# Hybrid trunk step on one Trainium2 core: each 1 MB piece of w_mod asked for as four transfers of 512 columns

## The chip, the cores and the metric

The kernel runs on 1 core of one Trainium2 chip. Its engines are TensorE (in the profile PE, and PEld for its weight loads), VectorE (DVE), ScalarE (ACT), GpSimd (POOL) and SyncE (SP), which here only asks for transfers. 16 DMA engines move the data. The time is the device time of one execution in microseconds; three runs of the kernel before gave 1928.62 to 1929.17, median 1928.89.

## The reference

One inference step of a two-layer trunk over two groups of tokens (128 context tokens, 512 latent tokens, 1024 features) in float32. Layer 0 mixes by windowed attention and a gated DeltaNet in both directions, layer 1 by latent attention; each is followed by a convolution FFN. All norms are modulated by a map of the conditioning vector:

```python
def trunk_layer(l, x, cvec, prm, ctx):
    mod = jax.nn.silu(cvec) @ prm["w_mod"][l] + prm["b_mod"][l]
    shift1, scale1, gate1, shift2, scale2, gate2 = jnp.split(mod, N_MOD, axis=-1)
    h = rmsnorm(x, prm["norm_pre"][l, 0]) * (1.0 + scale1) + shift1
    ...                                   # mix: even_mixer (l = 0) or odd_mixer (l = 1)
    x = x + gate1 * rmsnorm(mix, prm["norm_post"][l, 0])
    h = rmsnorm(x, prm["norm_pre"][l, 1]) * (1.0 + scale2) + shift2
    f = conv_ffn(h, prm["ffn_w_up"][l], prm["ffn_conv"][l], prm["ffn_w_down"][l])
    return x + gate2 * rmsnorm(f, prm["norm_post"][l, 1]), new_ctx
```

`w_mod` is (2, 1024, 6144): 50 MB, the largest tensor. The DeltaNet of layer 0 runs in chunks with a triangular inverse in each:

```python
    t_inv = lax.linalg.triangular_solve(a + eye, eye, left_side=True, lower=True, unit_diagonal=True)
    u = t_inv @ (vc * bc[..., None])
    w = t_inv @ (kb * jnp.exp(gc)[..., None])
```

## The kernel before, in words

The order of all work is written out by hand for each engine; engines meet by semaphores. Activations lie with features on partitions, tokens along the row. Weight blocks of 128 output columns come through two raw buffers, are split into a high and a low part by ScalarE and VectorE, and TensorE multiplies three times per block (`proj`, L2007).

`w_mod` is worked on in two places. The first 2048 columns of layer 0 (`w_mod_first`, eight pieces, one per 128 input rows) come at the start. The other 10240 columns, five rounds of eight pieces, are spread over the delta steps, from 229 to 431 us. A piece is 128 partitions by 2048 columns, a row of 8 KB, thus 1 MB. Four buffers `MW` (`w_mod_raw`) lie in the memory of the raw weight buffers, free in that stretch. Piece u goes to buffer u % 4. SyncE (`mod_load`, L626 to L631) waits until TensorE is done with piece u - 4 (`mod_done`) and asks for it in one transfer, which adds 16 to `mod_landed{u % 4}` when all of it is there. The first eight pieces of the program have added 16 to the same semaphores once.

TensorE uses a piece with silu(c) as the weights: `mod_part` (L2211) in one go, four matmuls of 512 columns; `mod_half` (L2220) in two halves of four times 256. These stand as filler between the steps of the delta ladder. There are five delta rounds r, each with two chains c (forward and backward), and in each a ladder of levels `lv` that inverts the triangular matrix: TensorE multiplies 64 x 64 blocks (L2398, then L2451 and L2454), VectorE masks and adds (L1700, L1706, L1709), TensorE goes on. `mod_first_half` waits for a piece and does one half between L2398 and L2451; `mod_piece(halved=True)` does the other after L2454. In rounds 1 to 4 three whole pieces stand together at the start of the round, so three slots come free within 2 us and SyncE asks for three pieces there. The code of this stretch has no loops: each instruction stands once in memory. After the last piece SyncE asks for the blocks of `ev_w_out`.

Of the kernel before, what the change touches and what calls it, by code (L numbers as in the profile page):

```python
# [27 lines left out]
D = 1024  # L28
KD = D // P
# [79 lines left out]
def build(nc, a, outs):  # L109
# [14 lines left out]
    def S(name):  # L124
        if name not in sems:
            sems[name] = stack.enter_context(nc.semaphore(name))
        return sems[name]
# [41 lines left out]
    def place(name, shape, off, dt=F32):  # L169
        return nc.alloc_sbuf_tensor_at(name, [P] + shape, dt, offset=BASE + 4 * off)  # L170
# [121 lines left out]
    MSLOTS = 4  # L292
    MW = [place(f"w_mod_raw{s}", [2 * D], R_RAW + s * 2 * D) for s in range(MSLOTS)]
# [154 lines left out]
    def mod_columns_of(i):  # L448

        return (i + 1) // 3, 2 * D * ((i + 1) % 3)  # L450
# [105 lines left out]
    with stack:  # L556
# [4 lines left out]
        def _(sp):  # L561
# [39 lines left out]
            wm = [a["w_mod"][l].rearrange("(k p) m -> p k m", p=P) for l in range(2)]  # L601
# [24 lines left out]
            def mod_load(u):  # L626

                if u >= MSLOTS:
                    sp.wait_ge(S("mod_done"), KD + u - MSLOTS + 1)
                l, m0 = mod_columns_of(u // KD)  # L630
                sp.dma_start(MW[u % MSLOTS][:, :], wm[l][:, u % KD, m0:m0 + 2 * D]).then_inc(S(f"mod_landed{u % MSLOTS}"), 16)  # L631
            for u in range(MSLOTS):
                mod_load(u)
            for u in range(MSLOTS, MPARTS):
                mod_load(u)
# [1364 lines left out]
        def _(pe):  # L2000
# [207 lines left out]
            def mod_part(w, k, b):  # L2208

                for j in range(4):  # L2210
                    last = pe.matmul(PS[32 * j:32 * j + 32, b * 512:b * 512 + 512], SCX[:, k, :], w[:, 512 * j:512 * j + 512],  # L2211
                                     start=(k == 0), stop=(k == KD - 1))
                last.then_inc(S("mod_done"), 1)

            def mod_half(w, k, b, x):

                n = 2 * P
                for j in range(4):
                    c0 = 512 * j + n * x
                    last = pe.matmul(PS[32 * j:32 * j + 32, b * 512 + n * x:b * 512 + n * x + n], SCX[:, k, :], w[:, c0:c0 + n],  # L2220
                                     start=False, stop=(k == KD - 1 and x == 1))
                if x == 1:
                    last.then_inc(S("mod_done"), 1)

            def mod_turn(n, rows, b):

                pe.wait_ge(S("mod_rows"), n)
                for j in range(4):
                    last = turn(PS[:, b * 512 + P * j:b * 512 + P * j + P], rows[:, P * j:P * j + P])
                last.then_inc(S("mod_turned"), 1)  # L2230
# [75 lines left out]
            def mod_first_half(r, k):  # L2306

                u = KD * r + k
                pe.wait_ge(S(f"mod_landed{u % MSLOTS}"), 16 * (u // MSLOTS + 2))
                mod_half(MW[u % MSLOTS], k, 6, 0)  # L2310

            def mod_piece(r, k, halved=False):

                u = KD * r + k
                if k == 0 and r > 0:
                    pe.wait_ge(S("a_rotated"), r)
                    mod_turn(r + 1, MROW, 7)
                if halved:
                    mod_half(MW[u % MSLOTS], k, 6, 1)
                else:  # L2320
                    pe.wait_ge(S(f"mod_landed{u % MSLOTS}"), 16 * (u // MSLOTS + 2))
                    mod_part(MW[u % MSLOTS], k, 6)

            def v_turn(x):
# [45 lines left out]
            for r in range(NT):  # L2370
# [30 lines left out]
                if r == 0:  # L2401
                    v_turn(0)
                else:
                    for c in range(2):
                        pe.wait_ge(*both("eg", c, r + 1))
                    for k in range(3):
                        mod_piece(r, k)
                for lv in range(LEVELS - 1):
# [24 lines left out]
                    if lv == 0:  # L2433
                        if r == 0:
                            mod_piece(r, 0)
                        continue
                    if lv in (4 + e, 5 + e) and r < NT - 1:
                        k_times_state(r, lv - 4 - e)
                    elif r == 0 and lv < 5 or r > 0 and lv < 4:
                        mod_first_half(r, lv + 2 * (1 - e))  # L2440
# [16 lines left out]
                    if r == 0 and lv < 5 or r > 0 and lv < 4:  # L2457
                        mod_piece(r, lv + 2 * (1 - e), halved=True)
                    elif r == 0:
                        mod_piece(r, 5)  # L2460
                    elif lv == 4:
                        mod_first_half(r, 6)
                    else:
                        mod_piece(r, 6, halved=True)
# [15 lines left out]
                if r == 0:  # L2480
                    k_times_state(r, 1)
                else:
                    mod_first_half(r, LEVELS)
# [328 lines left out]
```

## Time and profile before

| | |
|---|---|
| median of 3 runs | 1928.89 us (1928.62 to 1929.17) |
| the profiled execution: its time | 1928.23 us |
| its span, first to last instruction | 1926.4 us |
| granted TensorE clock, mean | 0.993 |
| TensorE busy | 1841.1 us, 96% of the span |
| VectorE, ScalarE, GpSimd busy | 963.8, 827.9, 55.0 us |
| transfers `w_mod_raw<-in_w_mod` | 40 of 1024 KB, median 6.9 us to landing |
| read from HBM, written | 165.08 MB, 3.44 MB |

The profile is of one execution. "Busy" counts the union of an engine's instructions; a matmul's end is modelled. A wait "<- issue" is idle time of an engine that no semaphore in the profile explains. A wait "<- DMA" was ended by a transfer that landed. The DMA share is the mean busy share of the 16 DMA engines; in a short window it can pass 1.00, since a packet counts in the window in which it starts. A packet is what one DMA engine moves as one piece of contiguous memory.

### The profile page before, as it was taken

To read this page: it belongs to the slowest core of one execution; us is meant where nothing else is said; L and a number is where in the kernel's file an instruction comes from. 1 tells how busy PE (TensorE), PEld (TensorE's weight loads), DVE (VectorE), ACT (ScalarE), POOL (GpSimd) and SP (SyncE) were. 2 spreads that over 40 slices of the span, in tenths; PEclk is the share of its full clock that TensorE was granted. 3 is DMA by queue.
4 is the path that set the end of the run, shared out by engine and by line. 5 is a ranking of instruction groups with operands and counts; after the bars stand their busy time and mean duration, and the time that the engine had idled before them with its cause. 6 is when DMAs were issued, how large, how long until landed. Compare 5 with 4: busy or idle time off the path is not lost.

```text
span 1926.4 us, 36263 instructions
## 1 busy us (share of the span) xinstructions
PE 1841.1 (96%) x14824; PEld 1698.8 (88%) x14824; DVE 963.8 (50%) x1613; ACT 827.9 (43%) x1420; POOL 55.0 (3%) x76
## 2 busy tenths in 40 slices
PE   6999998888899999999999999999999999999998
PEld 3999966667799999999999887776899999999997
DVE  4433355556746655235555743344375553255555
ACT  4545422225745544124445653343464441244453
POOL 0000122220000000000000000000000000000000
PEclk9999999998999999999999999999999999999999
DMA  7222366531021223222234311110211232122243
GB/s 284 65 58 66 128 252 221 199 141 51 1 71 44 77 71 87 71 66 68 73 94 140 95 44 32 27 35 28 67 44 55 76 87 78 55 76 76 78 136 115
DMA packets 238723, 170.23 MB, mean 88 GB/s; under 512 B 20139, under 2 KB 230285, under 8 KB 232333
## 3 DMA queue, kind: packets, MB, share of 16 engines
q1 hardware_dynamic: 238604, 168.54, 28.2%
q8 instruction: 88, 1.44, 0.3%
q14 instruction: 31, 0.25, 0.0%
HBM read 165.08 MB, written 3.44 MB: 87 GB/s over the span
## 4 chain that ended last, share of the span: by engine, by line
PE 85%; DVE 6%; ACT 4%; issue 3%; DMA 1%; SPq 0%; ACTq 0%; DVEq 0%
PE ps L2007 46%; PE ps L2083 15%; PE ps L2040 4%; PE ps L2201 3%; PE ps L2708 2%; PE ps L2745 2%; PE ps L2704 2%; PE ps L2398 1%; PE ps L2220 1%; PE ps L2578 1%; PE ps L2451 1%; PE ps L2555 1%; PE ps L2211 1%; PE ps L2028 1%; ACT w_hi L782 1%
## 5 line engine op out<-in xcount | busy, mean ns | idle before, releaser
L782 ACT ACTIVATE w_hi<-w_raw 128x1024 fp32r<-128x1024 f32 (+4 forms) x187 | 198.6, 1062 | 559.6 <-PE ps L2007 436.0
L1366 DVE TENSOR_TENSOR w_lo<-w_raw,w_hi 128x1024 fp32r<-128x1024 f32 (+4 forms) x191 | 234.2, 1227 | 377.2 <-ACT w_hi L782 376.8
L2007 PE MATMUL ps<-h_hi,w_hi 128*128 128x322 f32 x1648 | 381.5, 313 | 3.2 <-ACT conv L972 1.7
L2007 PE MATMUL ps<-h_lo,w_hi 128*128 128x322 f32 x1648 | 380.2, 312 | 0.0
L2007 PE MATMUL ps<-h_hi,w_lo 128*128 128x322 f32 x1648 | 378.1, 310 | 0.0
L2007 PEld LDWEIGHTS ps<-h_hi,w_hi 128*128 128x128 f32 x1648 | 278.1, 189 | 4.8 <-ACT conv L1192 2.0
L2007 PEld LDWEIGHTS ps<-h_hi,w_lo 128*128 128x128 f32 x1648 | 279.1, 189 | 0.0
L2007 PEld LDWEIGHTS ps<-h_lo,w_hi 128*128 128x128 f32 x1648 | 279.1, 189 | 0.0
L2083 PE MATMUL ps<-g_hi,w_hi 128*128 128x322 f32 x352 | 110.7, 314 | 2.7 <-DVE g_lo L1850 1.6
L2083 PE MATMUL ps<-g_lo,w_hi 128*128 128x322 f32 x352 | 109.6, 311 | 0.0
L2083 PE MATMUL ps<-g_hi,w_lo 128*128 128x322 f32 x352 | 109.1, 310 | 0.0
L2083 PE MATMUL ps<-h_hi,w_out_hi 128*128 128x322 f32 x288 | 90.8, 315 | 0.0
L2083 PE MATMUL ps<-h_lo,w_out_hi 128*128 128x322 f32 x288 | 89.8, 312 | 0.0
L2083 PE MATMUL ps<-h_hi,w_out_lo 128*128 128x322 f32 x288 | 89.5, 311 | 0.0
L1837 DVE SCALAR_TENSOR_TENSOR conv<-u,vec_cols,conv 128x642 f32<-128x642 f32 x88 | 78.0, 886 | 12.5 <-ACT conv L1192 12.1
L1840 DVE SCALAR_TENSOR_TENSOR conv<-u,vec_cols,conv 128x642 f32<-128x642 f32 x88 | 78.1, 887 | 10.6 <-DVE conv L1837 0.6
L1197 ACT ACTIVATE g_hi<-gated 128x642 f32 (+1 forms) x44 | 32.6, 741 | 104.0 <-DVE gated L1848 104.0
L2083 PEld LDWEIGHTS ps<-g_hi,w_hi 128*128 128x128 f32 x352 | 66.3, 188 | 4.0 <-DVE g_lo L1850 2.2
L1192 ACT ACTIVATE conv<-ps,vec_cols 128x644 f32<-128x644 f32 x88 | 69.7, 792 | 0.0
L2083 PEld LDWEIGHTS ps<-g_lo,w_hi 128*128 128x128 f32 x352 | 66.4, 189 | 0.2
L2083 PEld LDWEIGHTS ps<-g_hi,w_lo 128*128 128x128 f32 x352 | 66.5, 189 | 0.0
L1868 DVE COPY f_t<-ps 128x644 f32 (+1 forms) x16 | 13.3, 829 | 100.9 <-PE ps L2007 82.3
(376 smaller groups left out, 3337.5 us busy)
## 6 DMA issues: line engine op xcount, KB each, us to landing
w_raw<-in_ffn_w_up SPq DMA_DIRECT2D x88, 512.0 KB, 3.7
w_mod_raw<-in_w_mod SPq DMA_DIRECT2D x40, 1024.0 KB, 6.9
w_raw<-in_ffn_w_down SPq DMA_DIRECT2D x48, 704.0 KB, 4.5
w_raw<-in_ev_w_in SPq DMA_DIRECT2D x18, 512.0 KB, 3.6
w_mod_first<-in_w_mod SPq DMA_DIRECT2D x8, 1024.0 KB, 15.6
w_raw<-in_ev_w_out SPq DMA_DIRECT2D x8, 512.0 KB, 4.3
w_raw<-in_od_w_out SPq DMA_DIRECT2D x8, 512.0 KB, 4.0
w_raw<-in_od_w_kv_up SPq DMA_DIRECT2D x24, 128.0 KB, 2.3
```

The source lines that it names most:

```text
L782: act.activation(WH[slot][:, 0:k, :], RAW[slot][:, 0:k, :], ACT.Copy).then_inc(w_hi, 1)
L1192: act.activation(halves(Y[b][:, :]), pair(b0 + 2 * slot), ACT.Copy, scale=vcol(v0 + b * FCH, j)).then_inc(evac_a, 1)
L1366: dve.tensor_tensor(WL[slot][:, 0:k, :], RAW[slot][:, 0:k, :], WH[slot][:, 0:k, :].bitcast(F32), ALU.subtract).then_inc(w_lo, 1)
L1837: dve.scalar_tensor_tensor(y[:, 1:643], u[:, 0:642], vcol(v0 + b * FCH, j), y[:, 1:643], ALU.mult, ALU.add).then_inc(S(f"f_conv{b}"), 1)
L1840: last = dve.scalar_tensor_tensor(y[:, 1:643], u[:, 2:644], vcol(v0 + b * FCH + 4 * FCH, j), y[:, 1:643], ALU.mult, ALU.add)
L2007: last = pe.matmul(out, w_of(k, wi), x_of(k, xi, i), start=(k == 0 and p == 0), stop=(k == ks - 1 and p == 2))
L2040: last = pe.matmul(bank(2 * slot + hf, HW), (WH, WL)[wi][slot][:, k, :], x[xi][:, k, hf * HW:(hf + 1) * HW], start=(k == 0 and p == 0), st ...
L2083: last = pe.matmul(out, w[wi][:, k, :], x[xi][:, k, tk(g)], start=(k == 0 and p == 0), stop=(k == ks - 1 and p == 2))
L2201: return pe.transpose(out, src, IDENT[0:rows, 0:rows])
L2704: return pe.matmul(area(s, k0, w), QPE[i % 2][half(s), tile], KPT[half(s), k0:k0 + w], start=True, stop=False)
L2708: return pe.matmul(area(s, k0, w), QN[h][:, tile], KN[h][:, k0:k0 + w], start=False, stop=True)
L2745: last = pe.matmul(COUT[:, P * s:P * s + P], VO[i % 2][:, s, kt_tile, :], pt, start=(x == 0), stop=(x == len(tiles) - 1))
```

## The change

`mod_load` asks for a piece in four transfers of 512 columns each (a row is then 2 KB), into the same buffer. All four add 16 to the piece's semaphore, so a piece adds 64, and TensorE's two waits count accordingly. The pieces of the first eight (`w_mod_first`) stay as they are, and so does every instruction of TensorE, VectorE, ScalarE and GpSimd.

```diff
--- before.py
+++ after.py
@@ -628,7 +628,9 @@
                 if u >= MSLOTS:
                     sp.wait_ge(S("mod_done"), KD + u - MSLOTS + 1)
                 l, m0 = mod_columns_of(u // KD)
-                sp.dma_start(MW[u % MSLOTS][:, :], wm[l][:, u % KD, m0:m0 + 2 * D]).then_inc(S(f"mod_landed{u % MSLOTS}"), 16)
+                for j in range(4):
+                    sp.dma_start(MW[u % MSLOTS][:, 512 * j:512 * j + 512], wm[l][:, u % KD, m0 + 512 * j:m0 + 512 * j + 512]
+                                 ).then_inc(S(f"mod_landed{u % MSLOTS}"), 16)
             for u in range(MSLOTS):
                 mod_load(u)
             for u in range(MSLOTS, MPARTS):
@@ -2306,7 +2308,7 @@
             def mod_first_half(r, k):
 
                 u = KD * r + k
-                pe.wait_ge(S(f"mod_landed{u % MSLOTS}"), 16 * (u // MSLOTS + 2))
+                pe.wait_ge(S(f"mod_landed{u % MSLOTS}"), 16 + 64 * (u // MSLOTS + 1))
                 mod_half(MW[u % MSLOTS], k, 6, 0)
 
             def mod_piece(r, k, halved=False):
@@ -2318,7 +2320,7 @@
                 if halved:
                     mod_half(MW[u % MSLOTS], k, 6, 1)
                 else:
-                    pe.wait_ge(S(f"mod_landed{u % MSLOTS}"), 16 * (u // MSLOTS + 2))
+                    pe.wait_ge(S(f"mod_landed{u % MSLOTS}"), 16 + 64 * (u // MSLOTS + 1))
                     mod_part(MW[u % MSLOTS], k, 6)
 
             def v_turn(x):
```

## Rows read from the trace of the kernel before

**Rows 1.** The page: all packets; the instruction queue: packets, MB, share.
```profile
DMA packets 238723, 170.23 MB, mean 88 GB/s; under 512 B 20139, under 2 KB 230285, under 8 KB 232333
q8 instruction: 88, 1.44, 0.3%
```

**Rows 2.** Waits of TensorE, 225 to 445 us: who <- what: us, times, longest.
```profile
PE ps L2454 <- issue: 5.0, 4, 1.7
PE ps L2220 <- issue: 2.2, 2, 1.2
PE ps L2398 <- issue: 1.4, 1, 1.4
PE ps L2211 <- DMA w_mod_raw<-in_w_mod: 1.0, 1, 1.0
PE ps L2451 <- issue: 0.8, 1, 0.8
PE ps L2220 <- DMA w_mod_raw<-in_w_mod: 0.3, 1, 0.3
```

**Rows 3.** Chain that ended last, 225 to 445 us: start, us, what.
```profile
229.81 8.92 DMA w_mod_raw<-in_w_mod
289.00 1.71 issue
415.56 1.18 issue
```

**Rows 4.** Timeline at 291.2 us: start, us, instruction [idle before <- what ended it].
```profile
291.18 0.29 DVE L1706 TENSOR_TENSOR r_blocks<-r_blocks,ps 128x128 f32<-128x128 f32 x1 [1.96 <-PE ps L2454]
```

**Rows 5.** Instruction queue in the 0.1 us from 288.4, 414.4 and 421.98: packets, MB, share.
```profile
q8 instruction: 1, 0.02, 60.1%
...
q8 instruction: 1, 0.02, 54.9%
...
q8 instruction: 1, 0.02, 62.4%
```

**Rows 6.** Windows: length, PE PEld DVE ACT POOL busy (xcount), PEclk, DMA share, GB/s.
```profile
234.00:241.50 7.50, 6.20 (x189) 3.92 (x189) 3.85 (x12) 4.89 (x14) 6.76 (x6) 1.00 1.01 426
1921.00:1922.00 1.00, 0.68 (x6) 0.68 (x7) 0.27 (x1) 0.00 (x0) 0.00 (x0) 1.00 1.07 412
34.50:36.00 1.50, 1.50 (x12) 0.21 (x8) 0.06 (x1) 1.38 (x2) 0.00 (x0) 0.50 1.14 346
285.27:289.05 3.78, 3.73 (x140) 2.69 (x134) 2.19 (x9) 0.00 (x0) 2.88 (x3) 1.00 1.01 425
411.80:415.60 3.80, 3.74 (x126) 2.70 (x125) 1.97 (x8) 0.00 (x0) 2.92 (x3) 1.00 1.02 349
416.74:421.30 4.56, 4.55 (x125) 2.87 (x127) 1.33 (x4) 0.00 (x0) 0.00 (x0) 1.00 0.31 115
```

**Rows 7.** Queues and issues in 405 to 409.6 us; all packets in 280 to 288.4.
```profile
q1 hardware_dynamic: 154, 1.15, 70.4%
q8 instruction: 1, 0.02, 1.2%
w_mod_raw<-in_w_mod SPq DMA_DIRECT2D x3, 1024.0 KB, 7.7
...
DMA packets 383, 2.88 MB, mean 343 GB/s; under 512 B 32, under 2 KB 32, under 8 KB 32
```

**Rows 8.** SyncE's issues (start, us), then a wait of its in the whole run.
```profile
8.09 3.96 SPq L603 DMA_DIRECT2D w_mod_first<-in_w_mod  x8
...
SPq L631 <- PE ps L2220: 95.5, 20, 8.9
```

**Rows 9.** Pieces: all 40 to landing; the one of 280.05; its first use.
```profile
DMA to landing us min/median/max: 4.7/6.9/12.6
...
DMA to landing us min/median/max: 5.1/5.1/5.1
...
287.43 0.42 PE L2220 MATMUL ps<-w_mod_raw,silu_c 128*32 128x256 f32 x4
```

## The prediction

> **What bounds the kernel now.** I read the page first: a span of 1926.4 us and TensorE busy for 96% of it and 40 transfers `w_mod_raw<-in_w_mod` of 1 MB each (all in the table above). A change in how these land can only matter where TensorE waits, so next come its waits in the stretch of the delta steps, 225 to 445 us. The reader is to see two kinds there. It waits for the pieces themselves twice, 1.0 and 0.3 us. And it waits for "issue" eight times: 5.0 + 2.2 + 1.4 + 0.8 = 9.4 us [rows 2]. Third, the chain that ended last, same stretch: the second piece's landing is on it, and so are the issue waits, up to 1.71 us [rows 3]. Each of them stands inside the serial ladder of small matmuls that feeds VectorE level by level: VectorE waits 1.96 us for TensorE across the longest of them [rows 4].
>
> "Issue" only says that no semaphore explains the wait. The DMA queues do: beside the data queue there is one of kind instruction, with 88 packets and 1.44 MB, thus 16 KB each [rows 1]. In 0.1 us windows from 288.4 and 414.4 us lies one such packet each [rows 5], and TensorE's waits of 1.71 and 1.18 us end at 290.7 and 416.7 us [rows 3]: both times 2.3 us after the packet began. So TensorE ran out of instructions. From where it resumed at 411.8 to where it stopped at 415.6 it took 126 matmul and 125 weight-load records; from 416.74 to 421.30 it took 125 and 127 and did not stop [rows 6]. Blocks of some 250 instructions, then, one fetched while the one before runs. What differs is when the fetch starts. In the second case it starts at 421.98 to 422.08, alone in its window [rows 5], 0.7 us after the next block was entered. In the first, with pieces moving at a DMA share of 1.02, it starts at 414.4, 2.6 us after the block was entered. At 288.4 it is 3.1 us after the block entered at 285.27. The excess, 1.9 and 2.4 us, is time spent behind the packets of the pieces: I call it the queueing of a fetch.
>
> **The change part by part.** Nothing moves on any compute engine. SyncE asks four times instead of once per piece, for 120 more issues; the bytes stay.
>
> *SyncE.* Eight transfers of 1 MB asked for in a row took 3.96 us, 0.49 each. 120 more cost 59 us of a queue that waits 95.5 us for the matmuls of L2220 alone to free a slot [rows 8]. Hidden. Behind them in this queue stand two small output stores and the `ev_w_out` loads, which wait for the last piece's use anyway. Cost 0.
>
> *Moving the bytes.* In 234 to 241.5 us, 8 KB packets alone, 426 GB/s at a share of 1.01: 422 at full share, a piece takes 1.049 MB / 422 = 2.48 us. Packets of 2 KB exist in this trace only as output stores, 412 at 1.07: 385, a piece 2.72 us, a quarter 0.68. Packets of 512 B give 346 at 1.14: 303, a piece 3.45 us [rows 6]. Bounds: +0 and +0.97 us a piece; I take the store's row, the same size, +0.24.
>
> *Where later landing shows.* Pieces 0 and 1 are waited for already, in a burst in which the DMA engines are full. Their landings move by 0.24 and 0.48 us, and the second carries the first: +0.5 us on the chain (bounds 0 and 2 × 0.97 = 1.9). The issues don't bind there: the chain has the second piece asked for at 229.81 and landed at 238.73 [rows 3]; eight quarters from 229.3 are asked for by 233.3, a piece lands 4.7 us after its issue at the least [rows 9], 2.2 beyond its 2.48, so the last quarter could be there at 233.3 + 2.2 + 0.68 = 236.2. Later rounds: the tightest use is at 287.43, of the piece asked for at 280.05 and landed 5.1 us later [rows 9]; 2.3 us of room, against at most 3 × 0.49 = 1.5 us if the last quarter's issue binds. Cost 0.
>
> *The fetches.* This is the term that decides. In 405.0 to 409.6 us three pieces were asked for; by its end a fetch has started and the data queue has begun 1.15 MB, little more than the 1.05 of one piece [rows 7]: the fetch gets in ahead of nearly all of the two others. So a fetch waits for what an engine took up before it, and not for all that is asked for. If that is a transfer's share on the engine (8 rows, 2.48 us now) or a count of packets, it shrinks with the change to a quarter of a piece, 0.68 us, or from 310 to 85 ns a packet (8 KB at 26.4 and 2 KB at 24.1 bytes per ns and engine, the two rates above over 16). Queueing of 1.9 to 2.4 us becomes 0.5 to 0.7. For the wait that ended at 416.75: fetch at 411.8 + 0.7 + 0.5 = 413.0, ready at 415.3, needed at 415.56: gone. For the longest, 1.71 us: 285.27 + 0.7 + 0.7 = 286.7, ready at 289.0, needed at 289.00: just gone. The six others last 0.7 to 1.4 us, no more than the 1.4 to 1.7 us saved in queueing. Bounds: all 9.4 us go, or none does, and with 9% longer transfers each of the eight grows by 0.24, +2 us. I take all gone, by [rows 7]. Nothing is late in their place: VectorE sat idle behind the longest and went on at 291.18, 0.5 us after TensorE did [rows 4], so a stop that goes shortens the ladder by its whole length.
>
> The Trainium skill, "DMA: Bandwidth & Descriptors", Queues, rings and completion order, says that each DMA engine goes round its queue rows and drains a whole packet, typically 9 to 17 descriptors, before it switches. The trace agrees in so far as a fetch got in after about one piece in [rows 7]; by that rule the sum is the one below, and without it that of rival B. The same page, Bandwidth, advises batches of 1 MiB or more, with a fixed 2 us per transfer; paid one after another that would make a piece an estimated 10 us. Pieces queued together in 234 to 241.5 us pay nothing of the kind, so by these rows nothing of it enters the sum.
>
> **Sum**, against the profiled execution's 1928.2 us: 1928.2 - 9.4 + 0.5 = 1919.3. The median of the runs is 0.7 above it: 1920.0 us.
>
> **The rivals.**
> B, the fetch waits behind bytes. For it: at 288.4 three pieces had been asked for since 280.05, and of their 384 large packets about 350 had started (383 less the 32 small ones) [rows 7]. The fetch so got in before a last third of the third piece, at neither a transfer's end nor at once; an engine that takes up some 64 to 80 KB ahead would look like this, and 2 KB packets would not shorten it. Against it: nothing that these rows exclude. Then the eight waits stay, or grow by up to 0.24 us each: 1928.9 + 0.5 + 0 to 2 = 1929.4 to 1931.4, say 1930.5. That the change doesn't do what it says is no case of its own: [rows 1] show packets of 8 KB and over, 238723 - 232333 = 6390, about 48 pieces of 128, so they do become smaller; but if size is not what holds a fetch, it is this case.
>
> C, slower: fetches wait longer. Quarters that move at the 512 B rate, with a completion for each, take 3.45 us a piece; queueing behind bytes grows by 39%, about +1.0 us at each of the eight waits, and the first two pieces come 1.9 us late: 1928.9 + 8 + 1.9 = 1939. It decides once the growth is over (3.9 - 0.5) / 8 = 0.43 us a fetch, a full-share rate below about 360 GB/s on queueing of 2.5 us. For it: the stops are that tight, and 512 B packets show such a rate. Against: 2 KB stores show 385.
>
> **How the numbers follow.** What a measurement of this kernel can tell from no change is 0.2%, 3.9 us. A 0.50, B 0.37, C 0.13. A's own range is 1918 to 1925: a few of the marginal waits may stay in part. A counts as faster but for 0.02; B is within 0.2% in nearly all; C is slower. The range of 8 in 10 holds A and B: 1917.5 to 1932.
>
> **What would show it.** Right: issue waits on TensorE between 225 and 445 us fall from 9.4 us to under 2, and the fetch packets start within about 1.3 us of a block's start; the waits for `w_mod_raw` grow from 1.3 to about 1.8 us. A median time to landing that falls would not count by itself. Wrong: the eight issue waits at the same lines with the same lengths (B), or more of them (C); a full-share rate in the first burst far from 385 GB/s; SyncE issues of over 0.6 us each, or a wait for a piece after round 0.

## The result, and the profile after

The changed kernel takes 1935.3 us (median of 22 runs, 1928.2 to 1939.9) against 1929.1 (22 runs, 1923.0 to 1939.2) of the kernel before: ratio 1.0025, 95% interval 1.0014 to 1.0035. It is slower by a quarter of a per cent. The forecast was 1920.0, faster.

The profiled execution of the changed kernel took 1939.8 us (its span is 1938.0), 4.5 us over its median; the one of before 1928.2. Lines of the changed kernel are two higher than before (L2456 answers to L2454, L2400 to L2398, L2222 to L2220). First the page's packets and the instruction queue, which answer to [rows 1]:

```profile
DMA packets 256003, 170.25 MB, mean 88 GB/s; under 512 B 22058, under 2 KB 232204, under 8 KB 254732
q8 instruction: 88, 1.44, 0.3%
```

The change did what it says: 256003 - 254732 = 1271 packets of 8 KB and over are left of 6390. The instruction queue is the same to the packet. Now TensorE's waits in 225 to 445 us (who <- what: us, times, longest), which answer to [rows 2]:

```profile
PE ps L2456 <- issue: 7.2, 4, 2.6
PE ps L2400 <- issue: 2.5, 2, 2.0
PE ps L2453 <- issue: 1.9, 1, 1.9
PE ps L2213 <- DMA w_mod_raw<-in_w_mod: 1.2, 1, 1.2
PE ps L2222 <- DMA w_mod_raw<-in_w_mod: 1.1, 1, 1.1
```

The issue waits were to go. They grew from 9.4 to 11.6 us, and the waits for pieces from 1.3 to 2.3. Next, the longest of these stops in detail: the chain of the changed kernel around it (start, us, what), then three windows of that kernel (length, busy of PE PEld DVE ACT POOL, granted clock, DMA share, GB/s). The first is the burst of the first pieces, the second the block of code ahead of the stop, the third what follows it:

```profile
289.57 2.58 issue
...
293.80 2.01 PE ps L2346 x2
295.81 1.90 PE ps L2400 x32
```

```profile
234.00:241.50 7.50, 5.25 (x137) 3.25 (x139) 2.55 (x9) 3.80 (x12) 7.50 (x8) 1.00 0.99 343
285.84:289.57 3.73, 3.73 (x140) 2.69 (x134) 2.14 (x9) 0.00 (x0) 2.86 (x3) 1.00 0.95 286
291.70:298.50 6.80, 6.35 (x62) 3.19 (x61) 1.42 (x5) 0.00 (x0) 0.00 (x0) 0.50 0.90 322
```

The block entered at 285.84 us is the one of 285.27 before (x140, x134 in both, [rows 6]); TensorE is through with it 3.73 us later and stops, for 2.58 us where it was 1.71 [rows 3]. The fetch is this packet of the instruction queue, in the 0.1 us from 289.8:

```profile
q8 instruction: 1, 0.02, 60.0%
```

That is 4.0 us after the block's entry, where it was 3.1 at this place in [rows 5]. TensorE resumes at 292.15, again 2.3 us after the packet began. The same stop has a second price. The third window shows the granted clock at 0.50, TensorE's lower level of 1.2 GHz, and 62 matmuls in 6.8 us. The same place before in a window, and then two pieces of that kernel's chain (the first from an earlier round, the second from this place). The windows hold other matmuls in part, so it is the pieces that are compared:

```profile
291.00:297.80 6.80, 6.80 (x167) 4.59 (x162) 3.81 (x12) 0.00 (x0) 0.00 (x0) 1.00 0.74 231
```

```profile
251.35 1.10 PE ps L2344 x2
...
292.76 1.08 PE ps L2398 x32
```

Two matmuls of L2346 took 2.01 us against 1.10 for the two of L2344, 32 of L2400 took 1.90 against 1.08. So the clock is low behind the stop, and the ladder went on at about half speed. Through VectorE's eyes (its row answers to [rows 4], where it had waited 1.96 us):

```profile
292.83 0.29 DVE L1708 TENSOR_TENSOR r_blocks<-r_blocks,ps 128x128 f32<-128x128 f32 x1 [3.04 <-PE ps L2456]
```

The last view is SyncE's issues of the pieces (ns min/median/max) and their landing, which answer to [rows 8, 9]:

```profile
L632 SPq DMA_DIRECT2D w_mod_raw<-in_w_mod x160: 327/433/2214, 227.9 to 425.6; - x160
...
DMA to landing us min/median/max: 2.6/4.4/7.1
```

From the first to the last use of a piece, before took 194.8 us and after 208.4. Issue waits account for 2.2 of these 13.6 us and waits for pieces for 1.0. The rest, 10.4 us, is put down here to the 27.3 us with the clock at 0.5, of which before has none in this stretch; at half speed they can cost up to 13.7 us. Some of it comes back by chance right behind it: before has 17.1 us at 0.5 from 440.4 us, after 6.8. One profile of each is thus not enough to size the clock's part (second profiles are among the experiments).

### The profile page after: what moved, and what is told of

It is laid out like the page before. It is cut to its first block, busy times and chain, and to the rows that moved or that the text cites. A ratio compares the mean times of both kernels' runs of the same rounds, so it can differ in the third digit from the quotient of the medians.

```text
span 1938.0 us, 36383 instructions
## 1 busy us (share of the span) xinstructions
PE 1845.9 (95%) x14824; PEld 1701.2 (88%) x14824; DVE 963.8 (50%) x1613; ACT 827.5 (43%) x1420; POOL 54.9 (3%) x76
## 2 busy tenths in 40 slices
DMA packets 256003, 170.25 MB, mean 88 GB/s; under 512 B 22058, under 2 KB 232204, under 8 KB 254732
## 4 chain that ended last, share of the span: by engine, by line
PE 86%; DVE 6%; ACT 4%; issue 3%; DMA 1%; SPq 1%; ACTq 0%; DVEq 0%
PE ps L2009 45%; PE ps L2085 15%; PE ps L2042 5%; PE ps L2203 3%; PE ps L2710 2%; PE ps L2747 2%; PE ps L2706 2%; PE ps L2400 1%; PE ps L2222 1%; PE ps L2453 1%; PE ps L2580 1%; PE ps L2557 1%; PE ps L2213 1%; ACT w_hi L784 1%; DVE scores L1803 1%
## 5 line engine op out<-in xcount | busy, mean ns | idle before, releaser
L1842 DVE SCALAR_TENSOR_TENSOR conv<-u,vec_cols,conv 128x642 f32<-128x642 f32 x88 | 78.1, 888 | 10.6 <-DVE conv L1839 0.6
```

The costliest lines, as they stand in the source:

```text
L1842: last = dve.scalar_tensor_tensor(y[:, 1:643], u[:, 2:644], vcol(v0 + b * FCH + 4 * FCH, j), y[:, 1:643], ALU.mult, ALU.add)
```

## The experiments

Two theories went into the first batch: that fetches queue behind the bytes of the pieces (rival B's mechanism), and that the quarters cost something by being four. Each set of kernels has its own runs of the kernel before (medians 1928.6 to 1931.3), so ratios are compared, not times. "Late" is the start of a fetch's packet minus the entry of its block, the mean over the 30 blocks of the stretch, counted in steps of 256 TensorE records of the trace: 1.75 us before and 2.05 after. The instruction queue also carries fetches that are not TensorE's, so such a mean is good to some 0.3 us; where TensorE stopped, its fetch is certain, 2.2 to 2.4 us ahead of the end of the stop.

**No reloads.** Pieces 4 to 39 are not loaded; the four buffers are used as first filled.

```diff
-                sp.dma_start(MW[u % MSLOTS][:, :], ...).then_inc(S(f"mod_landed{u % MSLOTS}"), 16)
+                if u < MSLOTS:
+                    sp.dma_start(MW[u % MSLOTS][:, :], ...).then_inc(S(f"mod_landed{u % MSLOTS}"), 16)
```

> Leaves out 36 of the 40 transfers of the delta steps (every piece after the fourth is computed with what lies in the buffer). Theory 1 (fetches of TensorE's instructions queue behind the pieces, whatever the packet size): the issue waits of 9.4 us and the waits for pieces (1.3 us) are gone but for the first round's, no spell of low clock between 240 and 430 us, and the time is about 8 to 11 us under that of before. Theory 2 (the stops come from the fetch itself, at fixed places in the code): the issue waits stay where they are, and the time moves by less than 2 us.

Measured: 1916.0 us (6 runs), ratio 0.9923 [0.9905, 0.9942]. Its waits in the stretch:

```profile
PE ps L2221 <- DMA w_mod_raw<-in_w_mod: 0.4, 1, 0.4
PE ps L2221 <- issue: 0.2, 1, 0.2
```

Fetches are 0.76 us late and the stops are gone but for 0.2 us: the traffic of the pieces makes them. Together with the waits for pieces and the time at the low clock they are worth some 15 us, more than the 9.4 and 10.8 us of issue waits in the two profiles of before.

**One in flight.** One transfer a piece; from piece 4 on SyncE asks for piece u only when u - 1 has landed.

```diff
+                if u >= MSLOTS:
+                    sp.wait_ge(S(f"mod_landed{(u - 1) % MSLOTS}"), 16 * ((u - 1) // MSLOTS + 2))
```

> Packets and transfers as before (8 KB rows, one transfer a piece), but from the fifth piece on SyncE asks for a piece only when the one before has landed, so that at most one lies in a DMA engine's queue. Theory 1 (bytes taken up ahead hold the fetch): a fetch queues behind one share at most, 2.5 us, where bursts of three pieces gave up to 3.3; the issue waits fall from 9.4 to 4 to 7 us and the time by 2 to 5 us. Theory 2 (the queueing doesn't depend on what is asked for): issue waits and time as before.

Measured: ratio 1.0023 [1.0008, 1.0038]. Issue waits fell to 6.9 us, but TensorE waits 4.9 us for pieces, and the fetches are 2.2 us late on average. Fewer bytes at a time was no cure. The last batch shows why: this kernel asks for most of its pieces 1 to 2 us ahead of a block's entry, the worst place for them.

**Four transfers by rows.** The same 160 transfers, of 32 partitions with rows of 8 KB.

```diff
-                    sp.dma_start(MW[u % MSLOTS][:, 512 * j:512 * j + 512], wm[l][:, u % KD, m0 + 512 * j:m0 + 512 * j + 512]
+                    sp.dma_start(MW[u % MSLOTS][32 * j:32 * j + 32, :], wm[l][32 * j:32 * j + 32, u % KD, m0:m0 + 2 * D]
```

> Four transfers a piece as in the change, but cut by partitions (32 of them each), so rows stay 8 KB and packets 8 KB. If the number of transfers makes the change slower (completions, SyncE's longer issues): issue waits of 11 to 12 us and a time 4 to 6 us over before, as in the change. If the packet size does: issue waits near 9.4 us and the time of before within 2 us.

Measured: 1978.6 us, ratio 1.0247 [1.0226, 1.0269]. A window, and its longest waits in the stretch:

```profile
233.00:240.00 7.00, 4.36 (x104) 3.02 (x104) 2.93 (x8) 4.92 (x14) 6.23 (x6) 0.81 1.02 231
```

```profile
PE ps L2456 <- issue: 12.6, 6, 4.5
PE ps L2400 <- issue: 7.8, 2, 4.1
```

Full share gives 226 GB/s. The Trainium skill, "SBUF — State Buffer", Door 1: The DMA port swizzle, has a mapping of partitions to the memory's ports by which 32 neighbouring partitions reach 8 of the 16. The rate here, about half of the 422 GB/s of [rows 6], agrees. So this run does not isolate the number of transfers, but it tests the queueing hard: fetches are up to 6.8 us late.

**One transfer, 2 KB packets.** One transfer a piece into a buffer with a gap behind each 512 columns.

```diff
-    MW = [place(f"w_mod_raw{s}", [2 * D], R_RAW + s * 2 * D) for s in range(MSLOTS)]
+    MW = [place(f"w_mod_raw{s}", [4, 528], R_RAW + s * 2112) for s in range(MSLOTS)]
...
+                sp.dma_start(MW[u % MSLOTS][:, :, 0:512], wm[l][:, u % KD, m0:m0 + 2 * D].rearrange("p (j c) -> p j c", j=4)) ...
```

> One transfer a piece as before, but its rows go to four places 528 floats apart, so the packets are of 2 KB as in the change. If the packet size makes the change slower: issue waits of 11 to 12 us and 4 to 6 us over before. If the number of transfers does: as before within 2 us. Theory 1 in its form by bytes: queueing of fetches as before plus 9%, at most +2 us in issue waits.

Measured: 1935.1 us, ratio 1.0028 [1.0012, 1.0045], issue waits 12.2 us. The loss of the change comes with the packet size alone: the page has 20479 more packets under 8 KB than before, which is, but for one, 40 pieces of 512 packets. What 120 more issues and completions add is below what these intervals can tell, some 0.2%.

The second batch asked for the dose, and for the clock.

**Made stops.** No reloads, as above, and TensorE stops once a round for a small transfer it has asked for.

```diff
+                if k == 4:
+                    last.then_inc(S("mod_landed4"), 1)
+                    pe.wait_ge(S("mod_landed5"), 16 * (r + 2))
...
+            def stop_for(r):
+                sp.wait_ge(S("mod_landed4"), 17 + r)
+                sp.dma_start(STOP[:, :], wm[0][:, 0, 0:16]).then_inc(S("mod_landed5"), 16)
```

> As the run without reloads (36 of the 40 pieces are not loaded, which gave 0.9923 of the kernel before and no stops of TensorE), but in each of the five rounds TensorE is made to stop once, behind the first half of piece 4, until a transfer of 64 bytes a partition that it has asked for through SyncE has landed: a stop of known place and some 2.3 us, with the DMA engines idle. Theory 1 (a long stop is itself what makes the granted clock fall afterwards, and the slow matmuls are a second price on top of it): spells at 0.5 after most of the five stops, and the time is that of the run without reloads (1916) plus 5 x 2.3 plus 1 to 1.7 us for each spell, 1932 to 1936, ratio to before 1.001 to 1.004. Theory 2 (the clock falls for another reason, such as the traffic of the pieces, or in some executions only): no spell in the stretch, and 1916 + 11.5 = 1927.5 at most, ratio under 0.999.

Measured: ratio 1.0009 [0.9997, 1.0021], against 0.9923 without the stops: 0.0086 x 1929 = 16.6 us for five of them. The wait in the trace, and the windows behind three of them:

```profile
PE ps L2463 <- DMA stop_row<-in_w_mod: 10.3, 5, 3.0
```

```profile
253.80:257.20 3.40, 3.40 (x44) 2.60 (x37) 1.86 (x5) 0.00 (x0) 0.00 (x0) 0.50 0.02 5
291.30:294.70 3.40, 3.40 (x28) 1.69 (x26) 0.29 (x4) 0.00 (x0) 0.00 (x0) 0.50 0.02 5
376.60:380.00 3.40, 3.40 (x20) 1.12 (x22) 0.53 (x3) 0.00 (x0) 0.00 (x0) 0.51 0.02 5
```

With the DMA engines idle (share 0.02) the clock still falls behind a stop of 1.7 to 1.9 us. Half speed for 10.2 us costs 5.1; 10.3 + 5.1 = 15.4, and from first to last use of a piece this run takes 199.2 us against 183.7 without stops. So a stop of 2 us costs 3.1 to 3.3 on average. The other two stops, of 3.0 and 1.9 us, had no such spell: it doesn't follow every time. The stops were shorter than expected (1.7 to 1.9 us mostly), the spells three and not most of five, and the ratio came out just under the expected 1.001 to 1.004.

**Runs of 512 B, and 4 KB packets.** One transfer a piece in sixteen runs of 128 columns with gaps; and two transfers of 1024 columns.

```diff
+    MW = [place(f"w_mod_raw{s}", [16, 132], R_RAW + s * 2112) for s in range(MSLOTS)]
```

> One transfer a piece as in the kernel before, but rows land in sixteen runs of 512 bytes with a gap behind each, so the packets are of 512 bytes. Theory 1 (a fetch of instructions waits for a number of bytes taken up ahead of it, whatever the packets' size, so its price goes with the time per byte): at the 303 GB/s of such packets the queueing of 1.9 to 2.9 us grows by 39%, each of the eight stops by about 1 us, the clock falls after more of them; 1929 + 8 + 5 to 10 for the clock, ratio 1.007 to 1.012, issue waits of TensorE in the stretch 18 us or more. Theory 2 (it waits for a number of packets): 16 times smaller packets leave nothing of it, the issue waits go and the ratio is about 0.993 to 0.997. Theory 3 (the slowdown of the change has nothing to do with packets): ratio 1.000 to 1.003.

> Two transfers of 1024 columns a piece, packets of 4 KB: half way between the kernel before and the changed one. Theory 1 (time per byte decides): 4 KB packets move nearer to 8 KB than to 2 KB ones, so issue waits of 9 to 10 us and a ratio of 1.000 to 1.002, between the two kernels. Theory 2 (it is chance which kernel hits the stops, by where a fetch falls among the packets): any ratio from 0.998 to 1.004, with no order in size.

Measured: 1.0111 [1.0096, 1.0127] for the runs of 512 B and 1.0022 [1.0007, 1.0037] for 4 KB. The issue waits with 4 KB are 11.0 us; both this and the ratio are a little over what was expected of it. The waits with runs of 512 B, a window, and the packets of 233 to 241 us:

```profile
PE ps L2454 <- issue: 8.5, 6, 3.1
PE ps L2451 <- issue: 5.4, 3, 2.7
PE ps L2220 <- issue: 3.1, 3, 1.4
PE ps L2398 <- issue: 3.0, 2, 1.9
```

```profile
233.00:240.00 7.00, 4.52 (x140) 2.86 (x143) 3.09 (x8) 5.08 (x14) 6.14 (x7) 1.00 1.01 297
...
DMA packets 324, 2.37 MB, mean 296 GB/s; under 512 B 35, under 2 KB 35, under 8 KB 35
```

The packets did not become smaller. Of these 324 none lies between 512 B and 8 KB, and the page counts 238722 packets, one fewer than before: the rows in memory are still whole, only their places in the buffer are cut up. So this run can't tell a queue that counts packets from one that counts bytes, though its expectation says so, and a packet of the profile need not be contiguous at both ends. What it shows is the other half: the same packets, moved more slowly (445 ns each on average against 311), go with later fetches and longer issue waits, 20.3 us.

The count is settled by the kernels whose packets did shrink. In each, the largest delay in the first burst was taken, and what the data queue began between 0.5 us after the block's entry and the fetch: 1.37 MB in 182 packets before, 1.30 MB in 359 with halves, 1.30 MB in 653 with one transfer of 2 KB packets, 1.24 MB in 681 with the change. The packets grow fourfold in number and the bytes stay, so a fetch does not wait for a count of packets.

**Fifteen engines.** A piece as 120 and 8 partitions.

```diff
+                for p0, p1 in ((0, 120), (120, 128)):
+                    sp.dma_start(MW[u % MSLOTS][p0:p1, :], wm[l][p0:p1, u % KD, m0:m0 + 2 * D]) ...
```

> Each piece asked for as 120 partitions and as 8 partitions, rows of 8 KB as before. By the Trainium skill, DMA: Bandwidth & Descriptors, section on why a DMA increments its semaphore by 16, 120 partitions go to the fifteen lowest engines and 8 to the eight lowest, so the sixteenth DMA engine carries nothing of a piece; no run so far shows it. Theory 1 (the fetches of TensorE's instructions sit in the queue of one engine, and that is the last one): the fetches start within 0.7 us of their block in all rounds, the issue waits go, ratio 0.992 to 0.996, a version that beats both kernels. Theory 2 (they sit on another engine, or on several): the issue waits stay or grow by a sixteenth to an eighth of the queueing, ratio 1.000 to 1.004, and the longest queueing grows since eight engines carry nine rows instead of eight.

Measured: 1983.1 us, ratio 1.0294 [1.0276, 1.0312]. A window and its longest wait:

```profile
233.00:240.00 7.00, 3.79 (x98) 2.49 (x88) 2.65 (x7) 4.65 (x13) 6.53 (x6) 0.87 0.94 201
```

```profile
PE ps L2455 <- issue: 11.5, 4, 4.9
```

The share stands at 0.94, fifteen sixteenths, and most of the time 15 packets are under way in this window where it is 16 before. So one engine was left free by the pieces, as the page of the Trainium skill that the expectation names ("DMA: Bandwidth & Descriptors", Why a DMA increments its semaphore by 16 and not by 1) has it, and the fetches, up to 6.6 us late, did not go through it. Why the other fifteen move at half the rate stayed open.

All of these together, with the rate at full share in the first burst (GB/s over share) and issue waits in 225 to 450 us:

| kernel | GB/s | issue waits, us (times) | latest fetch, us | ratio |
|---|---|---|---|---|
| no reloads | - | 0.2 (1) | 3.0 | 0.9923 |
| before, 8 KB; two profiles | 418 | 9.4 (8), 10.8 (8) | 3.7, 3.9 | 1 |
| halves, 4 KB | 380 | 11.0 (8) | 4.1 | 1.0022 |
| one transfer, 2 KB | 385 | 12.2 (9) | 4.1 | 1.0028 |
| the change; two profiles | 346 | 11.6 (7), 11.8 (9) | 4.2, 4.5 | 1.0025 |
| one transfer, 8 KB in runs of 512 B | 294 | 20.3 (15) | 4.8 | 1.0111 |
| by rows | 226 | 31.5 (12) | 6.8 | 1.0247 |
| fifteen engines | 214 | 28.9 (11) | 6.6 | 1.0294 |

The 346 of the change is of one profile; the same window gives 359 in the second. Less the 0.5 us of a fetch that nothing holds up, the latest fetch times the rate is 1.3 to 1.4 MB in every row with reloads: 3.4 x 418, 3.6 x 385, 4.3 x 294, 6.3 x 226, 6.1 x 214. In these kernels a fetch waits for at most an estimated 80 to 90 KB on each of 16 engines, for packets of 8, 4 and 2 KB alike. The three kernels with 2 and 4 KB packets stand too near each other, in waits and in ratio, for an order among them.

**Paced.** If bytes ahead of a fetch make the stops, pieces should be asked for when no fetch is near. A first try held 24 pieces back until certain half pieces had been used, guided by the trace of before.

```diff
+                if u in gate:
+                    sp.wait_ge(S("mod_landed4"), 16 + first_halves(*gate[u]))
```

> The kernel before (one transfer a piece, packets of 8 KB), but SyncE doesn't ask for a piece as soon as its buffer is free: 24 of the 40 wait also for a first half of a later piece on TensorE, so that one piece at a time moves, each in the gap between two fetches of TensorE's instructions as the trace of before dates them. No buffer, instruction of TensorE or order of its work changes. Theory 1 (the stops are made by bytes of pieces that lie ahead of a fetch, at most 1.3 MB or so, and nothing else): the fetches start on average within 1 us of their block (1.75 before), at most two of the eight stops are left, issue waits under 3 us, no spell at the low clock, no wait for a piece over 0.5 us but for the first two; 1929 - 7 to -12 us, ratio 0.994 to 0.9965, faster than both kernels. Theory 2 (fetches are late for another reason too, or pieces asked for later come too late): the stops move to other places or become waits for w_mod_raw, ratio 0.999 to 1.003, as with one piece in flight.

> The same pacing in the changed kernel (four transfers of 512 columns a piece, packets of 2 KB). Theory 1 (2 KB packets cost only by what lies ahead of a fetch): with one piece at a time there is little ahead, and this kernel is within 0.15% of the paced one with 8 KB packets, ratio 0.994 to 0.998. Theory 2 (the quarters cost something of their own, by their issues or completions): it stays 0.25% or more above the paced one.

Measured: 0.9967 [0.9955, 0.998] and, with quarters, 0.9957 [0.9942, 0.9972], both faster than both kernels. The reason given was not borne out: issue waits were still 10.6 us in the first (4.8 in the second), fetches 2.2 us late in both. From first to last use of a piece the first took 200.1 us in its profile, more than before, so where its 0.3% comes from stays open.

This kernel also shows that 80 to 90 KB is no ceiling. Two pieces were asked for 1.4 and 1.0 us ahead of the block entered at 250.88 us; the fetch began 4.6 us after the entry, behind 1.7 MB or some 105 KB an engine, and TensorE stopped for 2.70 us. How deep a fetch stands in the queue depends on when the bytes were asked for.

**Both kernels again**, for second profiles.

> The kernel before once more, for a second profile of it: how much of its stops and of the granted clock is the same in another execution. Theory 1 (stops are set by where blocks and pieces fall, both fixed by the program; the clock afterwards is partly chance): about eight issue waits of 8 to 11 us in all at the same lines, fetches late by 1.6 to 1.9 us on average, and perhaps a spell or two at 0.5 after the longest stops, which makes up the spread of 1923 to 1939 us between runs. Theory 2 (the first profile was a lucky one): clearly more stops.

> The changed kernel once more, for a second profile. Theory 1: issue waits of 10.5 to 12.5 us in all, fetches late by 1.9 to 2.1 us on average, three to six spells at the low clock. Theory 2 (the first profile, at 1938 above the median of 1935, was an unlucky one): stops like those of the kernel before, and the difference would be in the spells alone.

Measured: 1927.0 and 1935.8 us, one execution each. Issue waits 10.8 and 11.8 us, waits for pieces 0.2 and 2.1, fetches late 1.78 and 2.11 us. At the low clock in the stretch: 3.4 us before, 13.6 after. So stops and lateness repeat; the time at the low clock does not, and the 27.3 us of the first profile of after were much.

**At the blocks' entries, and ahead of them.** In the paced trace the fetches were on time where a piece had been asked for at a block's entry, and 2.4 to 3.2 us late where one had been asked for 0.4 to 1.8 us ahead of it. So the increments were put on TensorE's matmuls right at the entries (the n-th calls, found by counting records), and for a control 24 calls earlier, some 1.5 us. A helper records the matmuls, so that they all have one line in these traces.

```diff
+            blocks = (3, 4, 5, 6, 7, 13, 14, 15, 16, 17, 21, 22, 23, 24, 25, 29, 30, 31, 32, 33, 36, 37, 38, 39)
...
+                if u in blocks:
+                    sp.wait_ge(S("mod_landed4"), 17 + blocks.index(u))
...
+            pe = Marked(pe, [1343, 1407, 1470, 1532, 1595, 1784, 1847, 1910, 1973, 2036, 2162, 2225, ...], S("mod_landed4"))
```

> The kernel before with 24 of the 40 pieces held back on SyncE until TensorE has entered a certain block of 256 instructions (an increment on a matmul within one or two of the block's first); one piece a block in the ladders. A fetch for the next block is asked for at the entry, the piece's bytes start some 1.5 us later and are through some 2.5 us after that, ahead of the next entry. Theory 1 (phase decides: bytes asked for before the fetch go ahead of it, bytes asked for after it do not): fetches late by 1.0 us or less on average, issue waits under 3 us in all in 225 to 445 us, a wait for a piece of up to 0.6 us in the last round, ratio 0.992 to 0.995. Theory 2 (any pacing gives the 0.3 to 0.4% that the first did, by a lower load): ratio 0.996 to 0.998, lateness about 2 us.

> The same in the changed kernel, four transfers of 512 columns a piece. Theory 1: with the phase right there is nothing ahead of a fetch whatever the packets' size, so within 0.15% of the one with 8 KB packets. The last quarter is asked for some 1.5 us after the first, which moves bytes towards the next entry: a stop or two of a few tenths of a us more. Theory 2 (quarters cost something of their own): 0.25% or more above it.

> As the first of these three, but each increment stands 24 calls of a matmul earlier, some 1.5 us ahead of the block's entry, so that a piece's bytes begin to move just when the fetch is asked for. The same number of pieces at a time and the same waits otherwise. Theory 1 (phase decides): fetches late by 2 to 2.5 us, eight or more stops, issue waits of 8 us or more, ratio 0.998 to 1.003. Theory 2 (pacing as such): the same ratio as the first within 0.15%.

Measured: 0.9912 [0.9892, 0.9931] at the entries (1914.3 us, 6 runs), 0.9926 [0.9907, 0.9945] with quarters (1917.1), and 1.0007 [0.9995, 1.002] with the same pacing 1.5 us earlier. The quarters' 2.8 us over the whole pieces go with 2.4 us of waits for pieces and 0.7 of issue waits, where whole pieces have none. The block that before entered at 285.27 us, in the kernel at the entries: windows of it and the next, and the fetch in the 0.1 us from 281.9.

```profile
281.28:284.77 3.49, 3.49 (x141) 2.56 (x135) 1.90 (x8) 0.00 (x0) 2.88 (x3) 1.00 0.62 195
284.77:289.40 4.63, 4.63 (x142) 2.91 (x134) 2.17 (x9) 0.00 (x0) 0.00 (x0) 1.00 0.88 311
```

```profile
q8 instruction: 1, 0.02, 86.4%
```

And ahead of the entries: the same block's window, a second window behind it, the stop in the chain, and the fetch in the 0.1 us from 287.7.

```profile
284.48:288.21 3.73, 3.73 (x140) 2.69 (x134) 2.13 (x9) 0.00 (x0) 2.85 (x3) 1.00 0.77 272
290.70:294.10 3.40, 3.40 (x28) 1.50 (x22) 0.31 (x3) 0.00 (x0) 0.00 (x0) 0.51 0.32 130
```

```profile
288.21 1.77 issue
```

```profile
q8 instruction: 1, 0.02, 60.1%
```

Piece 13 was asked for at 281.57, 0.3 us after the entry. Its first packets began 1.0 us after that, and the fetch 0.65 us after the entry, ahead of them: no stop. Asked for at 283.45, 1.0 us ahead of the entry at 284.48, its bytes were there first, the fetch began 3.3 us after the entry, and TensorE stopped for 1.77 us with 3.4 us at half clock behind it. Over the stretch: no issue wait at all and no wait for a piece, fetches 1.1 us late; against ten issue waits of 10.0 us, two waits for pieces of 1.4 us in all, fetches 2.2 us late. Phase decides, not load: in the ladders both kernels ask for the pieces one at a time. The rule has exceptions: ahead of the blocks entered at 296.24 and 300.78 us a piece was asked for 0.5 and 1.1 us early, and both fetches were on time all the same.

## Why the prediction was wrong

*What bounds it, where the stops come from*: right. "Issue" is a wait for a fetch behind the pieces' bytes; without the bytes it is gone but for 0.2 us (ratio 0.9923), and with the fetch ahead of them it is gone too (0.9912).

*SyncE, cost 0*: not refuted. Single issues took up to 2.2 us, which the prediction had named as a sign of being wrong, but no piece was waited for after round 0, and the one transfer with 2 KB packets is as slow as four.

*Moving the bytes, +0.24 us a piece*: the first burst gives 343 / 0.99 = 346 GB/s, 3.03 us a piece, so +0.55. The row of the stores (385) fits the single transfer with 2 KB packets, not the quarters. *First two pieces, +0.5 us*: too low. Waits for pieces grew by 1.0 and by 2.0 us in the two pairs of profiles, where the upper bound was 1.9.

*The fetches, -9.4 us*: this is the step that failed. It said that a fetch waits for a transfer's share or a count of packets, which shrinks to a quarter; its bounds of gain reached from all to +2 us, and it took all, by [rows 7]. The runs show a number of bytes, some 80 to 90 KB an engine with pieces asked for as they are in both kernels, as rival B had it from the 350 packets started at 288.4 us. Smaller packets carry these bytes more slowly, and the issue waits grow: +2.2 and +1.0 us in the two pairs. The rows could have told: "the fetch gets in ahead of nearly all of the two others" fits 64 to 80 KB as well as one piece's share of 64 KB, and between two readings of one number the sum took the one with the gain. The rule of the Trainium skill cited for it ("DMA: Bandwidth & Descriptors", Queues, rings and completion order: a whole packet of descriptors is drained before the engine switches) would have let the fetches in sooner with packets of 2 KB, if each of these is one descriptor; they came no sooner, in one transfer or in four.

*Rival B's time, 1929.4 to 1931.4*, was too low too. A term that neither the sum nor a rival had is the granted clock. Waits grew by 3.0 to 3.2 us in each pair of profiles, for a ratio worth 4.8 us (2.7 to 6.8). By the made stops, a stop of about 2 us costs half as much again in matmuls at half clock, and the changed kernel has more long stops: of 1.5 us and over, five against one in the first pair and five against two in the second. That this makes up the rest is thus likely, not shown: the difference itself is known to 2 us either way. The rows of the stretch in [rows 6] show the clock at 1.00 and gave no hint; none of the eight stops of before, 0.7 to 1.7 us, was followed by a fall in that one profile, one of eight in the second.

*Rival C* was to decide below a full-share rate of about 360 GB/s, and the rate was 346 and 359, so by its own condition C holds, and its direction is right. Its price of 10 us was not: it took the 303 GB/s of the 512 B packets, and the time came to about half of that. Nor was the rate of the quarters needed for the loss, since one transfer at 385 GB/s loses as much.

## What to carry to other kernels

In this kernel straight-line TensorE code is fetched over the same DMA engines as the data, in blocks of 16 KB. Where blocks of small matmuls last only some 3.4 to 4.7 us, ask for big transfers just after a block has been entered, not just before, and the stops go (here 0.9% of the time). The places were found by counting records of a trace, so they move with every edit of the code ahead of them. Splitting transfers or shrinking packets did not help: it makes the same bytes slower. Count a TensorE stop of 1.5 us or more at half as much again, for the clock may fall behind it, and take at least two profiles before sizing that part.

## What the runs showed of the hardware that was not expected

- In the kernels of the table the latest fetch waits for an estimated 80 to 90 KB per DMA engine, from 214 to 418 GB/s and with packets of 2, 4 and 8 KB alike; in a paced kernel it was some 105 KB. Bytes asked for up to 1.8 us before the block's entry mostly go first, those asked for at it do not.
- The granted clock was at 0.5 (1.2 GHz) for 3.4 or 6.8 us behind many stops of TensorE of 1.2 us and over, also with DMA idle (three of the five made stops), but not behind each: one of 3.0 us had none.
- Four transfers of 2 KB rows into one piece move at 346 and 359 GB/s, one transfer with the same packets at 385, 4 KB at 380. One transfer whose rows land in runs of 512 B keeps its 8 KB packets and moves at 294.
- 32 partitions a transfer (8 KB rows) move at 226 GB/s, 120 + 8 partitions at 214, both about half of the 418 of 128.
